# Keeping the routed input once by token, in fp32, and giving its second place to two expert weight buffers

## The reference

```python
def expert_choice_ffn(h, w_router, w_gate, w_up, w_down):
    B_, L, D = h.shape
    cap = EC_CAPACITY * L // N_EXPERTS
    aff = jax.nn.softmax((h @ w_router).astype(jnp.float32), axis=-1)
    top_aff, top_idx = lax.top_k(jnp.swapaxes(aff, 1, 2), cap)
    xe = jax.vmap(lambda hb, ib: hb[ib])(h, top_idx)
    hid = jax.nn.silu(jnp.einsum('becd,edf->becf', xe, w_gate)) * jnp.einsum('becd,edf->becf', xe, w_up)
    ye = jnp.einsum('becf,efd->becd', hid, w_down) * top_aff[..., None].astype(h.dtype)
    combine = lambda ib, yb: jnp.zeros((L, D), yb.dtype).at[ib.reshape(-1)].add(yb.reshape(-1, D))
    return jax.vmap(combine)(top_idx, ye)
```

## Time and profile before

| what | us |
|---|---|
| median of 3 runs (2705.84 to 2706.39) | 2706.21 |
| the profiled execution: its time | 2707.64 |
| its span, first to last instruction | 2705.8 |
| PE busy / share | 2567.9 / 95% |
| DVE, ACT, POOL busy | 1218.3, 708.2, 150.9 |
| bytes read from HBM | 376.28 MB |
| last expert weight chunk lands, on the span's clock | 2684.64 |

### The profile page before, as it was taken

One profiled execution on the slowest core, in us unless ns is written; L12 is line 12 of the kernel. 1 busy time (PEld: TensorE's weight loads), 2 busy tenths in 40 slices (PEclk: granted clock), 3 DMA queues, 4 the chain that ended last, 5 costly groups with the idle time before them and its releaser, 6 DMA issues.

```text
span 2705.8 us, 33779 instructions
## 1 busy us (share of the span) xinstructions
PE 2567.9 (95%) x14526; PEld 1680.1 (62%) x14526; DVE 1218.3 (45%) x1933; ACT 708.2 (26%) x1135; POOL 150.9 (6%) x102
## 2 busy tenths in 40 slices
PE   8999999999999999999999998999899979999997
PEld 4446677888885446677788885564888643444332
DVE  5963446533345974355533345423566431211212
ACT  2252242322222143243322224112322131111101
POOL 0000000000000000000000000800233110000000
PEclk9999999999999999999999998989999989999999
DMA  4334212224322224221323324111000319999997
GB/s 155 90 125 155 94 47 78 80 81 114 94 83 99 77 107 156 94 78 48 109 79 108 101 75 145 37 57 53 13 2 3 121 68 393 421 421 421 421 421 304
DMA packets 243386, 380.57 MB, mean 141 GB/s; under 512 B 21769, under 2 KB 182822, under 8 KB 218534
## 3 DMA queue, kind: packets, MB, share of 16 engines
q1 hardware_dynamic: 242876, 378.08, 38.9%
q10 hardware_dynamic: 362, 0.33, 0.0%
HBM read 376.28 MB, written 2.10 MB: 140 GB/s over the span
## 4 chain that ended last, share of the span: by engine, by line
PE 81%; DVE 8%; DMA 7%; ACT 3%; issue 1%; SPq 0%; DVEq 0%; ACTq 0%
PE banks L1025 33%; PE banks L960 9%; PE banks L1826 8%; PE banks L1408 7%; PE banks L1540 3%; PE banks L1008 2%; PE banks L1670 2%; DMA ring<-in_w_gate 2%; DMA arena<-in_w_gate 2%; DVE arena L2694 2%; PE banks L1064 1%; PE banks L1298 1%; PE banks L1012 1%; PE banks L1167 1%; PE banks L1272 1%
## 5 line engine op out<-in xcount | busy, mean ns | idle before, releaser
L2089 ACT ACTIVATE w_hi<-ring 128x2048 fp32r<-128x2048 f32 (+1 forms) x100 | 174.6, 1746 | 424.1 <-PE banks L1025 424.1
L2570 DVE TENSOR_TENSOR w_lo<-ring,w_hi 128x2048 fp32r<-128x2048 f32 (+1 forms) x96 | 198.7, 2069 | 148.2 <-ACT w_hi L2089 146.9
L1025 PE MATMUL banks<-ffn_x_hi,w_hi 128*128 128x512 f32 x640 | 249.0, 389 | 0.0
L1025 PE MATMUL banks<-ffn_x_lo,w_hi 128*128 128x512 f32 x640 | 249.0, 389 | 0.0
L1025 PE MATMUL banks<-ffn_x_hi,w_lo 128*128 128x512 f32 x640 | 249.0, 389 | 0.0
L2694 DVE SCALAR_TENSOR_TENSOR arena<-arena,taps 128x512 f32<-128x512 f32 x240 | 166.1, 746 | 2.5
L2896 DVE TENSOR_TENSOR squares<-gates,banks 128x512 f32<-128x512 f32 x44 | 30.2, 688 | 275.5 <-PE banks L1025 262.3
L1408 PE MATMUL banks<-zT,ring 128*128 128x512 f32 x320 | 146.2, 615 | 2.5 <-ACT zT L2219 1.7
L960 PE MATMUL banks<-xT,ring 128*128 128x512 f32 x320 | 139.1, 594 | 0.5 <-ACT taps L1965 0.5
L1025 PE MATMUL banks<-ffn_hidden_hi,w_hi 128*128 128x512 f32 x352 | 138.4, 393 | 0.0
L1025 PE MATMUL banks<-ffn_hidden_hi,w_lo 128*128 128x512 f32 x352 | 137.1, 389 | 0.0
(11 more groups left out here) (448 smaller groups left out, 4295.5 us busy)
## 6 DMA issues: line engine op xcount, KB each, us to landing
ring<-in_ffn_w_in SPq DMA_DIRECT2D x88, 512.0 KB, 5.1
ring<-in_w_down SPq DMA_DIRECT2D x30, 1024.0 KB, 24.5
arena<-in_w_gate SPq DMA_DIRECT2D x29, 1024.0 KB, 24.1
arena<-in_w_up SPq DMA_DIRECT2D x29, 1024.0 KB, 23.4
ring<-in_w_gate SPq DMA_DIRECT2D x26, 1024.0 KB, 23.1
ring<-in_w_up SPq DMA_DIRECT2D x26, 1024.0 KB, 23.8
arena<-in_w_down SPq DMA_DIRECT2D x26, 1024.0 KB, 25.8
ring<-in_w_mod SPq DMA_DIRECT2D x24, 1024.0 KB, 7.3
```

The costliest lines, as they stand in the source:

```text
L1025: mm = pe.matmul(bank[:, :], weights(wp, k), rhs(rp, k), start=(k == 0 and wp == rp), stop=(k == n - 1 and wp == 1))
L2089: nc.scalar.activation(hi[:, 0:m], raw[n % 2][:, 0:m], ACT.Copy).then_inc(f_hi.sem, 1)
L2570: ins = V.tensor_tensor(lo[:, 0:m], raw[n % 2][:, 0:m], hi[:, 0:m].bitcast(F32), ALU.subtract)
```

## The change

The tokens by row are kept once, in fp32, as `h_tok` in the place of the old `h_full`. ACT copies each turned step once. GpSimd's subtraction goes. `gather` multiplies in fp32: 4 products in place of 8 for each half. The 16 KB per partition of the old `h_tok_hi` (its place is that of `mix2`, the input of the output product) become two more buffers for expert chunks, numbers 12 and 13, so `EB` is 16; they are filled right behind chunks 10 and 11, under the same wait (`wo_ok` 8), and the two buffers in `xT` become 14 and 15. From then on chunk n waits for `e_used` to reach n - 15. Two semaphores of older work are used again for the two buffers.

```diff
-        h_tok = [rounded("h_tok_hi", arena_at + 4 * mix2_at, ST, D), rounded("h_tok_lo", arena_at + 4 * qT_at, ST, D)]
...
-        h_full = view(qT_at, ST, D)
+        h_tok = view(qT_at, ST, D)
...
-        e_w += ring_now[2:6] + [xT.rearrange("p a n -> p (a n)")[:, i * EC:(i + 1) * EC] for i in range(2)]
+        e_w += ring_now[2:6] + [view(mix2_at + i * EC, EC) for i in range(2)] + [xT.rearrange("p a n -> p (a n)")[:, i * EC:(i + 1) * EC] for i in range(2)]
         EB = len(e_w)
-        E_GATE, E_DELTA, E_HEADS, E_OUT, E_X = 0, 2, 7, 8, 12
+        E_GATE, E_DELTA, E_HEADS, E_OUT, E_X = 0, 2, 7, 8, 14
...
             def gather(q, hf):
                 aux.bank_free(pe, f"G{hf}", q)
                 pe.wait_ge(sel_ok, q + 1)
-                for i in range(2 * ST):
-                    t, part = i // 2, h_tok[i % 2]
-                    mm = pe.matmul(aux.bank(f"G{hf}", q), selq[:, t].rearrange("p j c -> p (j c)"),
-                                   part[:, t, hf * 512:(hf + 1) * 512], start=(i == 0), stop=(i == 2 * ST - 1))
+                for t in range(ST):
+                    mm = pe.matmul(aux.bank(f"G{hf}", q), selq[:, t].rearrange("p j c -> p (j c)").bitcast(F32),
+                                   h_tok[:, t, hf * 512:(hf + 1) * 512], start=(t == 0), stop=(t == ST - 1))
                 mm.then_inc(ax_mm, 1)
...
-            pe.wait_ge(ht_lo, 2 * ST)
+            pe.wait_ge(ht_ev, 2 * ST)
             pe.wait_ge(xtok_ev, 2 * ST)
...
-                for dst in (h_tok[0], h_full):
-                    A1(dst[:, n // 2, (n % 2) * 512:(n % 2 + 1) * 512], ps[2 + n % 6][:, :], ACT.Copy).then_inc(ht_ev, 1)
+                A1(h_tok[:, n // 2, (n % 2) * 512:(n % 2 + 1) * 512], ps[2 + n % 6][:, :], ACT.Copy).then_inc(ht_ev, 1)
...
-            for n in range(2 * ST):
-                pool.wait_ge(ht_ev, 2 * (n + 1))
-                cols = slice((n % 2) * 512, (n % 2 + 1) * 512)
-                G.tensor_tensor(h_tok[1][:, n // 2, cols], h_full[:, n // 2, cols], h_tok[0][:, n // 2, cols].bitcast(F32),
-                                ALU.subtract).then_inc(ht_lo, 1)
```

More of the change, by code:

```diff
@@ L547, in build @@
         rt_mm, rt_v, rt_a = sem("router_mm"), sem("router_vec"), sem("router_act")
-        ht_mm, ht_ev, ht_lo = sem("h_turned"), sem("h_high"), sem("h_low")
+        ht_mm, ht_ev = sem("h_turned"), sem("h_by_token")
         xtok_mm, xtok_ev = sem("x_turned"), sem("x_by_token")
@@ L552, in build @@
         e_used = sem("expert_chunk_used")
-        E_IN_BEFORE = [(rope_v, 10), (rope_s, 2), (p2_mm, 2), (cond_ok, 2), (const_in, 32), (x_in[0], 16), (x_in[1], 16), (mem_in, 16), (turned, 12), (turned_out, 12), (rows_in, DEPTH * 17 * 16)] + [(s, DEPTH * 16 * SPLIT_CHUNKS) for s in raw_in]
+        E_IN_BEFORE = [(ctx_loaded, 16), (p2_ev, 2), (rope_v, 10), (rope_s, 2), (p2_mm, 2), (cond_ok, 2), (const_in, 32), (x_in[0], 16), (x_in[1], 16), (mem_in, 16), (turned, 12), (turned_out, 12), (rows_in, DEPTH * 17 * 16)] + [(s, DEPTH * 16 * SPLIT_CHUNKS) for s in raw_in]
         ex_silu, ex_hid = sem("expert_silu"), sem("expert_hidden")
@@ L1735, in _ @@
                 if n >= 6:
-                    pe.wait_ge(ht_ev, 2 * (n - 5))
+                    pe.wait_ge(ht_ev, n - 5)
                 if n == 1:
@@ L1753, in _ @@
                 if n < 6:
-                    pe.wait_ge(ht_ev, 2 * (n + 3))
+                    pe.wait_ge(ht_ev, n + 3)
                 else:
```

## The result

The changed kernel takes 2710.12 us (median of 12 executions, 2708.51 to 2712.8) against 2705.78 (12, 2702.13 to 2709.07). The ratio is 1.0019, with a 95% interval of 1.0010 to 1.0028: slower, by 4.3 us between the medians and by 5.1 by the ratio, which is taken over all executions; 7.4 was forecast.

A forecast was written before the change was run, and what follows sets the result against it. PE bounds the expert loop until DMA takes over near the end; 17.4 us of waits for weights go and 24.8 us of PE work come, +7.4, so 2713.6 us for the median, 8-in-10 range 2708.5 to 2717.

The forecast's parts named there:

- main case: Whole kernel: PE bounds to the end with the clock about as now, 2711.7 to 2715.5 us, chance 0.60.
- Exp earlier by one copy: Router's Exp on ACT: one copy ahead of its table load goes, so the first selection matrix comes 0.49 us earlier.
- first gather to first chunk: First gather, ahead of the expert loop: in fp32, partly at low clock, 9.95 us in place of 6.55, +3.4.
- a gather in the loop: Each of seven gathers in the expert loop: fp32 takes 6.87 us instead of 3.74, +3.13 each, +21.9 in all.
- first chunk to last: Expert loop on PE: 21.9 us of gather work come and 17.4 us of waits for weights go, +4.5.
- first chunk to last landing: Weight stream from PE's first chunk at 2234.3 to the last chunk's landing at 2684.6: 450.3 us.
- forecast's own clock case: Pair 0 of the expert loop: if its low-clock stretch, costing PE 1.7 us, doesn't come, the time is 2711.9 us.
- a queue that runs dry: Weight stream behind the loop's first gather: a chunk issued 3.1 us later loses about 2.1 us there once.
- signs of being wrong: In the new profile: pairs under 57.3 us apart, chain ending in DMA pieces, or first chunk before 2233 or after 2238.
- DMA as the bound: End of the expert loop: the last chunk's landing still decides, -2.1 to 0 us, 2704 to 2706; chance 0.07.
- Fp32 as cheap as fp32r: Gathers: fp32 stays at 3.7 us, so DMA decides, -5.5 us, 2700.7; chance 0.04.
- The clock: PE-bound loop: low-clock stretches decide, 2708.8 to 2718.7 us; chance 0.20 for more high clock, 0.09 for more low.

The follow-up runs named there:

- e8: The changed kernel unaltered, measured again against the kernel before in a later comparison: 2714.37 us, ratio 1.0031.
- e9: Changed kernel plus 11 products of constants on PE in its wait for the routing, repeat of e3 for a second trace: 2711.11 us, one execution.
- e10: Changed kernel plus 11 products of constants on PE in its wait for the routing, repeat of e3 for a third trace: 2715.4 us, one execution.
- e1: Changed kernel with 14 chunk buffers as before, so only the fp32 gather is left of the change: 2714.68 us, ratio 1.0026 against the kernel before.
- e3: Changed kernel plus 11 products of constants on PE in its wait for the routing: 2713.38 us, ratio 1.0026 against the kernel before.
- e11: e3 plus one constant product ahead of the first gather and one in the first expert's wait for its hidden: 2709.54 us, ratio 1.0009.

## Why the prediction was right, and where it was off

The mechanism was right: all of the waiting for weights went, PE became the bound of the whole loop, and what the fp32 gather adds came out larger than what the buffers could give. By the ratios the kernel is slower by 5.1 us in the first comparison and by 8.4 in the second (0.31% of 2704.5), and the forecast's 7.4 lies between them and inside both intervals. By the medians alone it was 3 us too large in the first. Of the two outcomes that I weighed, slower by over 0.2% and within it, the first comparison (0.19%) falls just inside the second, to which I gave 0.28. Its median of 2710.12 lies in the range for 8 in 10 but under the main case's own, 2711.7 to 2715.5; e8's 2714.37 lies in that. Which of the two came first was chance.

Step by step, from the two traces:

| step | forecast | trace |
|---|---|---|
| Exp earlier by one copy | -0.49 | -0.48: from the start of the router's product to the table load 7.13 in place of 7.61 |
| first gather to first chunk | +3.4 | 2228.97 - 2215.92 = 13.05, before 2231.39 - 2221.97 = 9.42: +3.6 |
| a gather in the loop | +3.13 | 7.07 - 3.92 = +3.15 |
| pairs apart | 58.3 | 58.30 |
| first chunk to last | +4.5 | 458.19 - 455.25 = +2.9 |
| behind the last chunk | 0 | 19.84 - 19.16 = +0.7 |
| first chunk to last landing | 2684.6 - 2234.3 = 450.3 | 2676.7 - 2228.97 = 447.7, before 453.3 |
| last chunk landed before its use | 7 us | 8.5 us |
| ahead of the routing | 0 | -5.6 |

- **The price of fp32** was right to 0.02 us, since the trace had a row of the same shape and types. By the rule of four passes for true fp32 (the Trainium skill, "FP8 and Floating Point Precision", TensorE Precision Notes) it would have been +3.7, 0.6 more than the trace has.
- **First chunk to last.** The forecast has 1.6 more than the trace. On that side stand the 1.7 of the stretch of low clock that stood in the first pair of before and doesn't stand in this execution: the first pair is 2279.04 - 2228.97 = 50.07 in place of 48.64, +1.43 where +3.13 was to come. That is the forecast's own clock case (2711.9). 0.36 go the other way, in the one pair that takes 58.66 (2453.93 to 2512.59); the rest, some 0.2 on the side of the 1.7, is spread over the last pair and the last four chunks. The pair in the same place of before has the same short stop of PE, and I had taken my 55.16 from the three pairs ahead of it.
- **The last landing.** The two buffers took 5.5 us out of the stream of weights. The 2.1 us that I had added for a queue that runs dry behind the first gather of the loop don't show: the last landing came 2.6 us sooner behind the first chunk than forecast. Nothing hung on this term, since PE is the bound.
- **The tail** I had put at nothing. The clock falls in it at 2689.7, 2.6 us behind the last chunk; the combining products then run at 0.43 us in place of 0.23. In e9 and e10, whose clock stays up through those products, the tail is 19.2 us, as in the kernel before.
- **Ahead of the routing** nothing was changed, yet this trace is 5.6 us shorter there. The mean of the clock shows little of it (0.980 here, 0.977 in the kernel before, 0.978 in e8). At 205 to 210 us the changed kernel's first trace runs at full clock and e8, the same kernel, at half; at 340 to 345 they have 0.87 and 0.52. Set side by side product by product, e8 falls behind by 1.5 us at about 20 us, by 2.7 more between 203 and 206 and by 0.8 more at 335, each time where its clock is low and the other's is not:

```profile
205.00:210.00 5.00, 4.64 (x27) 2.65 (x23) 1.97 (x9) 3.49 (x11) 0.00 (x0) 1.00 0.89 315
340.00:345.00 5.00, 5.00 (x20) 4.02 (x20) 5.00 (x9) 4.44 (x6) 0.00 (x0) 0.87 0.02 3
```

```profile
205.00:210.00 5.00, 5.00 (x19) 0.86 (x18) 1.23 (x6) 0.13 (x1) 0.00 (x0) 0.50 0.17 24
340.00:345.00 5.00, 3.28 (x12) 2.73 (x13) 3.56 (x7) 2.40 (x4) 0.00 (x0) 0.52 0.00 0
```

So the part that the change touches costs -0.48 + 3.63 + 2.94 + 0.68 = +6.8 us in the trace, against +7.4, and the step that failed is one that the forecast didn't have: it took everything ahead of the change as equal between two executions. Executions of one kernel lie up to 7 us apart (the kernel before ranges from 2701.7 to 2709.5 over all comparisons), which is as large as the effect. For the same reason one of the forecast's own signs of being wrong came true without its cause: the first chunk began at 2228.97, before 2233. Behind the first gather it began 13.05 us later, and the forecast had 2234.3 - 2221.5 = 12.8.

Two readings in the prediction were off, and nothing hung on them. In the last fifth of the page's slices DMA stands at 9 in six of eight, not in all: the first of the eight is 1, the last 7. And a first gather at low clock throughout would cost 2 x 6.87 - 6.55 = +7.2, not +6.8, so the bound behind it is +6.7.

**The rivals.** DMA as the bound: excluded by the chain, which has no DMA in this part, and by e1. Fp32 as cheap as fp32r: excluded by the 7.07 us. The clock: it was the right thing to weigh, in both directions. With no low clock in the part (e3's and e11's traces) it is 3.1 us shorter than in the changed kernel's traces; with two stretches of it (e9, e10) it is 1.8 us longer.

## What to carry to other kernels

Buffers for weights are worth at most the time that the chain spends waiting for weights, here 17.4 us, and an edit that pays for them with work on the engine ahead has this much to spend: 8 gathers at 3.1 us were 25. Ask for the room in another way; two bf16 parts took the same room as one fp32 copy, left the gather as fast as it was, and the same two buffers then brought 0.27%. And where a change moves the bound from DMA to PE, every short stretch of low clock, which the wait for DMA had absorbed, comes into the time.

## What the runs showed of the hardware

- Two executions of one kernel give the same length to a hundredth of a microsecond in one part (471.24 and 471.24 from first gather to last chunk) and differ by 5.6 us in another, through stretches of the lower clock that one has and the other hasn't. The Trainium skill, "TensorE: Matmul & The Clock Gate", Part 1, says that the gate runs freely and doesn't restart with the kernel. The traces agree as far as they go: at 205 us the same program is at full clock in one execution and at half in the other.
- PE's clock fell though PE was busy: in e10's window at 2252 it is at 1.2 GHz with PE busy throughout, behind a wait of 1.02 us for the hidden and products with 16 rows of weights. In e3's trace the same wait and the same products stand in the same place, and the clock stays at 2.4 GHz. In e11's, with one product of constants in that wait, it stays up too; which of the two, the product or the execution, kept it there is not shown.
- A gather of 16 products, 128 by 128 weights and 512 columns, takes 3.92 us in fp32r and 3.56 in bf16 at 2.4 GHz; in fp32, 8 products take 7.07 and show as 16 rows.
- One core read weights from HBM at 421 GB/s, for 400 us on end (2272 to 2672 in the kernel before, with a DMA share of 1.01).
